# Layer 0's first steps by token tile: the first weight piece loaded between the two tiles

## The chip, the cores and the metric

The kernel runs on one core of a Trainium2 chip. Its time is the device time of one execution in microseconds (us). Before the change the median of three runs is 1185.62 us (1185.45 to 1185.66). The median is the number that a change is judged by.

## The reference

The program is a two-layer language-model body on 256 tokens of width 1024. Each layer normalizes the tokens (RMS norm with a gain per feature), multiplies them by one wide input matrix `w_in`, sends slices of the product through four mixers (an mLSTM, a latent attention, a gated linear attention and a convolution), fuses them with `w_out`, and adds a feed-forward part: dense in layer 0, a mixture of eight experts in layer 1. All of it is in float32.

```python
for l in range(DEPTH):
    z = rms_norm(h, norm1_g[l]) @ w_in[l]
    (m_qk, m_v, m_o, m_if, a_cq, a_ckv, a_kr,
     g_q, g_k, g_v, g_r, g_a, c_glu) = split_cols(z, IN_SPLITS)
    y = concat([mlstm_mixer(...), mla_mixer(...), gla_mixer(...), conformer_conv(...)])
    h = h + group_rms_norm(y, fuse_g[l], N_GROUPS) @ w_out[l]
    u = rms_norm(h, norm2_g[l])
    h = h + (swiglu(u, ...) if l % 2 == 0 else moe_ffn(u, ...))
return rms_norm(h, final_norm_g)
```

The change touches only the first line of layer 0: `rms_norm(h, norm1_g[0])` and the first columns of its product with `w_in[0]`.

## The kernel before, in words

The 256 tokens are two tiles of 128 (t = 0, 1); `h` holds them in SBUF. Every engine has its own program, written out by hand in order, and engines wait for each other by semaphores. Nothing reorders them: an instruction that waits holds all that stands behind it on its engine.

A float32 product is made of three products in a rounded format. Each operand is split into a high part and a low part. For weights, ScalarE (ACT) copies a piece from the ring of loaded pieces into `high` (`split_high`, L870) and VectorE (DVE) or GpSimd (POOL) subtracts to get `low` (L1353 on DVE, L675 on POOL). For tokens, the normalized tile `un` is transposed by TensorE (PE) into a PSUM bank in four groups of two blocks (L1947). ACT then writes `uTh` with the gain (L904) and DVE writes `uTl` (L1370), group by group (`tile_gains`).

`w_in` comes in pieces, in the order l0, l1, b, a, mq, mk, gqk, rg0, rg1, vo0, vo1. Pieces l0 and l1 hold the same 376 columns: l0 five of the eight blocks of 128 features, l1 the other three. For each token tile PE makes 15 matmuls of 376 columns with l0 and 9 with l1 (`half("l0", 0)` is tile 0 with l0, and so on; L2150 to L2152). Pieces b, a, mq, mk are feature-major: each half is 24 matmuls of 256 columns (L1965 to L1967) that need both tiles.

The order before, in layer 0, on each engine:

- SP issues the loads: x of tile 0, x of tile 1 (L545), then the pieces of `w_in`, each as two DMAs (L492). Ahead of piece 4 (mq) it waits for eleven small DMAs of POOL (`rows_in`).
- ACT: sum of squares and rstd of tile 0, then of tile 1 (`tile_rstd`, L885 to L890); gains of tile 0, groups 0 and 1; `high` of l0; gains of tile 0, groups 2 and 3; gains of tile 1; `high` of l1; `high` of b; three mask copies (L1011); `high` of a; copies of the first product (L1020, L1022); `high` of mq; the gates (L1026 to L1030).
- DVE: `normalize` of tile 0 and tile 1 (L1361); low gains of tile 0, groups 0 and 1; `low` of l0; the other low gains; `low` of l1; `low` of b.
- PE: the 8 transposes of tile 0, the 8 of tile 1, nine matmuls of the identity (L2125, which keep the engine active until the first weights are ready), `half("l0", 0)`, `half("l0", 1)`, `half("l1", 0)`, `half("l1", 1)`, two transposes of constants (L2252, L2253), then b, a matmul with `walpha` (L2267), small transposes, a, and the rest.
- POOL: constants, the small DMAs of `rows_in` and `gate_b`, then a wait for `norm_tr` to reach 8, which is the count of transposed groups of both tiles:

```python
pool.wait_ge(s["norm_tr"], steps_before(3 * l + 1))
pool.dma_start(walpha[:, :], gla_w_alpha[l]).then_inc(s["ukv_in"], 16)
```

Behind that wait stand five DMA issues (L698 to L702), the rotary angles (`angles`, L638 to L660: a chain of small operations in which nearly every one waits for the one before), and then `low` of piece a, `low` of mq and so on (`split_low`, L675). PE waits for `low` of a ahead of `half("a", 0)`.

The banks of the transposes are `START_BANKS[0]`; a bank is claimed again only when the reader of its last content is done.

Of the kernel before, what the change touches and what calls it, by code (L numbers as in the profile page):

```python
# [25 lines left out]
ACT = mybir.ActivationFunctionType  # L26
# [3 lines left out]
P = 128  # L30
# [104 lines left out]
def build(nc, x, positions, norm1_g, w_in, mlstm_conv_w, mlstm_conv_b, mlstm_gate_b,  # L135
# [25 lines left out]
    with ctx:  # L161
# [219 lines left out]
        UP_BANKS, GATE_BANKS = (0, 1), (4, 7)  # L381

        UP_FIRST, GATE_FIRST = (6, 3), (2, 5)
        START_BANKS = (((2, 0, 1, 4), (3, 5, 7, 6)), ((0, 1, 4, 7), (3, 4, 7, 0)))
        SPLIT_BANKS = ((0, 1, 4, 2), (0, 1, 4, 7))
        DENSE_ACC, MOE_ACC = ((2, 3), (5, 6)), ((2, 3),)

# [94 lines left out]
        def _(sp):  # L482
# [58 lines left out]
                                  w.rearrange("(k p) n -> p k n", p=P)[:, k0:k0 + 4, c * WIDE:c * WIDE + 256])  # L541
                                 for g, w in enumerate((wg, wu))], rounds)

            for t in range(TT):
                sp.dma_start(h[:, t, :], x[0, t * P:(t + 1) * P, :]).then_inc(s[f"x{t}_in"], 16)  # L545
            for p in range(N_IN):
                if p == 4:

                    sp.wait_ge(s["rows_in"], 16 * 11)
                load_in(0, p)  # L550
# [309 lines left out]
        def _(act):  # L860
# [11 lines left out]
            def tile_rstd(t, k=None, squares=un, halves=False):  # L872

                if halves:
                    for i in range(2):
                        act.wait_ge(s["h_ready"], 4 * k + 2 * t + i + 1)
                        at = slice(i * 512, (i + 1) * 512)
                        chain.done(act.activation(squares[:, t, at], h[:, t, at], ACT.Square, accum_out=ss[:, t, i:i + 1]))
                    chain.wait()
                    chain.done(act.activation(ss[:, t, 1:2], ss[:, t, 1:2], ACT.Copy, scale=1.0 / D, bias=EPS))  # L880
                    bias = ss[:, t, 1:2]
                else:
                    if k is not None:
                        act.wait_ge(s["h_ready"], 4 * k + 2 * t + 2)
                    chain.done(act.activation(squares[:, t, :], h[:, t, :], ACT.Square, accum_out=ss[:, t, 0:1]))  # L885
                    bias = epst[:, :]
                chain.wait()
                chain.done(act.activation(lnv[:, t, 0:1], ss[:, t, 0:1], ACT.Ln, bias=bias, scale=1.0 / D))
                chain.wait()
                act.activation(rstd[:, t, 0:1], lnv[:, t, 0:1], ACT.Exp, scale=-0.5).then_inc(s["rstd_ready"], 1)  # L890
# [7 lines left out]
            def tile_gains(k, first, t, banks, steps=range(4)):  # L898

                for g in steps:  # L900
                    act.wait_ge(s["norm_tr"], steps_before(k) + 4 * t + g + 1)
                    for i in range(2):
                        kd = 2 * g + i
                        last = act.activation(uTh[:, kd, t * P:(t + 1) * P], bank[banks[t][g]][:, i * P:(i + 1) * P],  # L904
                                              ACT.Copy, scale=col(first + kd))
                    last.then_inc(s["uth_ready"], 1)
# [63 lines left out]
            for l in range(DEPTH):  # L970
                n0 = LAYER_PIECES[l]
                def split_in(name):
                    split_high(n0 + IN_AT[name], width=in_width(name))
# [7 lines left out]
                if l:  # L981
                    split_in("l0")
                    act.preload_act_table_set(LN_EXP)
                    tile_rstd(0, 1, halves=True)
                    split_in("l1")
                    tile_gains(3 * l, NORM1 + KD * l, 0, START_BANKS[l])
                    tile_rstd(1, 1, halves=True)
                    n = n0 + IN_AT["b"]
                    act.wait_ge(loaded[SLOT_OF[n]], 32 * FILL_OF[n])
                    act.wait_ge(s["piece_used"], n - SPLIT + 1)  # L990
                    act.activation(high[:, n % SPLIT, 0:PIECE // 2], slot(n)[:, 0:PIECE // 2], ACT.Copy).then_inc(s["b_half"], 1)
                    tile_gains(3 * l, NORM1 + KD * l, 1, START_BANKS[l])
                    act.activation(high[:, n % SPLIT, PIECE // 2:], slot(n)[:, PIECE // 2:], ACT.Copy).then_inc(s["high_ready"], 1)
                else:
                    act.wait_ge(s["ident_ready"], 1)
                    for t in range(TT):
                        act.wait_ge(s[f"x{t}_in"], 16)
                        tile_rstd(t)
                    act.wait_ge(s["cols_ready"], 1)
                    tile_gains(0, NORM1, 0, START_BANKS[0], (0, 1))  # L1000
                    split_in("l0")
                    tile_gains(0, NORM1, 0, START_BANKS[0], (2, 3))
                    tile_gains(0, NORM1, 1, START_BANKS[0])
                    split_in("l1")
                if l:
                    split_in("a")
                else:
                    split_in("b")
                    act.wait_ge(s["consts"], 1)
                for out_, in_ in ((ident_r, ident), (mask_kr, mask_kt), (mask_qr, mask_qt)):  # L1010
                    last = act.activation(out_[:, :], in_[:, :], ACT.Copy)  # L1011
                last.then_inc(s["masks_ready"], 1)
                if l == 0:
                    split_in("a")
                else:

                    act.wait_ge(s["rows_written"], ZEROED)

                act.wait_ge(s["tile_done"], 3 * l + 1)
                act.activation(zl[:, 0, :], bank[PAIR_BANKS["l"][0]][:, 0:376], ACT.Copy).then_inc(s["zl_ready"], 1)  # L1020
                used("l1")
                act.activation(zl[:, 1, :], bank[PAIR_BANKS["l"][1]][:, 0:376], ACT.Copy).then_inc(s["zl_ready"], 1)  # L1022
                split_in("mq")

                act.wait_ge(s["gates_in"], l + 1)
                chain.done(act.activation(gab[:, :, :], gb[:, :, 4:8], ACT.Abs))  # L1026
# [319 lines left out]
        def _(dve):  # L1346
# [9 lines left out]
            def normalize(l, t):  # L1356

                dve.wait_ge(s["rstd_ready"], 4 * l + t + 1)
                for i in range(2):
                    at = slice(i * 512, (i + 1) * 512)  # L1360
                    dve.tensor_scalar(un[:, t, at], h[:, t, at], rstd[:, t, 0:1], None, ALU.mult).then_inc(s["un_ready"], 1)  # L1361

            def tile_gains(k, first, t, banks, steps=range(4)):

                for g in steps:
                    dve.wait_ge(s["uth_ready"], steps_before(k) + 4 * t + g + 1)
                    for i in range(2):
                        kd = 2 * g + i
                        at = slice(t * P, (t + 1) * P)
                        last = dve.scalar_tensor_tensor(  # L1370
                            out=uTl[:, kd, at], in0=bank[banks[t][g]][:, i * P:(i + 1) * P], scalar=col(first + kd),
                            in1=uTh[:, kd, at].bitcast(F32), op0=ALU.mult, op1=ALU.subtract)
                    last.then_inc(s["utl_ready"], 1)
# [57 lines left out]
            for l in range(DEPTH):  # L1431
# [7 lines left out]
                if l:  # L1439
                    split_in("l0")  # L1440
                    add_tile(0, DENSE_ACC[0], "dense_half", 1)
                    normalize(l, 0)
                    tile_gains(3 * l, NORM1 + KD * l, 0, START_BANKS[l], (0, 1))
                    add_tile(1, DENSE_ACC[1], "piece_used", DENSE0 + N_FFN)
                    tile_gains(3 * l, NORM1 + KD * l, 0, START_BANKS[l], (2, 3))
                    normalize(l, 1)
                    tile_gains(3 * l, NORM1 + KD * l, 1, START_BANKS[l])
                else:
                    dve.wait_ge(s["cols_tr"], 1)
                    dve.tensor_copy(cols[:, 2, :], bank[7][:, 0:P]).then_inc(s["cols_ready"], 1)  # L1450
                    normalize(0, 0)
                    normalize(0, 1)
                    dve.wait_ge(s["cols_ready"], 1)
                    tile_gains(0, NORM1, 0, START_BANKS[0], (0, 1))
                    split_in("l0")
                    tile_gains(0, NORM1, 0, START_BANKS[0], (2, 3))
                    tile_gains(0, NORM1, 1, START_BANKS[0])

                chain.done(dve.memset(vaug[:, :, :, DH:DH + 1], 1.0))
                if l:  # L1460
                    dve.wait_ge(s["moe_in"], 16)
                    dve.tensor_tensor(router[:, :, :], router[:, :, :], bc(cols[:, 0, NORM2 + KD:NORM2 + 2 * KD].unsqueeze(2), [P, KD, E]),
                                      ALU.mult).then_inc(s["router_ready"], 1)
                if l == 0:
                    split_in("l1")
                if l:

                    n = n0 + IN_AT["b"]
# [460 lines left out]
        def _(pe):  # L1929
# [184 lines left out]
            for l in range(DEPTH):  # L2114
# [3 lines left out]

                if l == 0:
                    start_transposes(0, 0)  # L2120
                    start_transposes(0, 1)

                    pe.wait_ge(*owner[0])
                    for _ in range(9):
                        pe.matmul(bank[0][:, 0:P], ident[:, :], ident[:, :], start=True, stop=True)  # L2125

                def half(name, i, reader=None, ahead_of_last=None):

# [113 lines left out]
                if l:  # L2242
                    half("l1", 0, ahead_of_last=lambda: start_transposes(l, 1, (0, 1)))
                    start_transposes(l, 1, (2, 3))
                half("l0", 1, ("zl_ready", 2 * l + 2))
                if l == 0:
                    half("l1", 0)
# [340 lines left out]
```

## Time and profile before

| what | value |
|---|---|
| median of three runs | 1185.62 us |
| the profiled execution | 1185.43 us |
| its span | 1183.5 us |
| PE busy | 1163.9 us, 98% of the span |
| DVE busy | 943.5 us, 80% |
| ACT busy | 835.4 us, 71% |
| POOL busy | 297.9 us, 25% |
| PE's share of the chain that ended last | 93% |
| first weight matmul (L2150) | starts at 13.39 us |

The span runs from the first to the last instruction of the profiled execution; the execution's own time is 1.93 us longer. The chain that ended last is followed backwards from the last instruction to what released it at each step. A row of the timeline gives the start, the length, the engine, the line, the operation and, in brackets, the idle time before it with what ended it; "x4" means four instructions merged in one row.

### The profile page before, as it was taken

The page shows a single profiled execution, that of the slowest core. Times are in us where ns is not written, and L with a number is a line of the kernel's source. Part 1 is how long each engine was busy: PE and PEld are TensorE (multiplying, and loading weights), DVE is VectorE, ACT ScalarE, POOL GpSimd, SP SyncE. Part 2 cuts the span into 40 slices and gives each one's busy share as a digit, 9 for nine tenths or more (in the row PEclk, how much of TensorE's full clock was granted, in tenths as well). Part 3 has the DMA queues.
Part 4 walks back from the last instruction along what each step waited for, and adds up shares of the span by engine and source line. Part 5 has one row for each costly group of instructions (what it writes and reads, how often), then busy time and mean ns, then how long its engine had stood idle before and what let it go on. Part 6 is the DMA issues. An engine that isn't in the chain of part 4 may idle for free.

```text
span 1183.5 us, 17063 instructions
## 1 busy us (share of the span) xinstructions
PE 1163.9 (98%) x5916; PEld 968.5 (82%) x5916; DVE 943.5 (80%) x868; ACT 835.4 (71%) x880; POOL 297.9 (25%) x301
## 2 busy tenths in 40 slices
PE   7999999999999999999999999999999999999996
PEld 7987888888888778888888888888888888888885
DVE  4875554455597579998899898899899899889997
ACT  7786634434768767777787777777777777778775
POOL 9976000000597654412003003003003003000000
PEclk9999999999999999999999999999999999999999
DMA  9544975625254499999999999999999999999971
GB/s 308 181 147 158 395 271 180 210 53 178 66 180 131 160 344 393 380 390 393 389 391 394 388 386 389 369 383 376 387 383 370 387 371 380 392 369 370 394 291 55
DMA packets 173846, 358.98 MB, mean 303 GB/s; under 512 B 15136, under 2 KB 46042, under 8 KB 173793
## 3 DMA queue, kind: packets, MB, share of 16 engines
q1 hardware_dynamic: 167600, 344.17, 80.0%
q0 software_dynamic: 6016, 13.84, 3.5%
q8 instruction: 32, 0.52, 0.2%
q10 hardware_dynamic: 176, 0.27, 0.1%
q14 instruction: 22, 0.17, 0.0%
HBM read 352.18 MB, written 9.70 MB: 306 GB/s over the span
## 4 chain that ended last, share of the span: by engine, by line
PE 93%; DVE 3%; ACT 2%; issue 1%; DMA 1%; SPq 0%; DVEq 0%; ACTq 0%
PE bank L2003 17%; PE bank L2005 17%; PE bank L2004 17%; PE bank L2023 8%; PE bank L2022 8%; PE bank L2021 8%; PE bank L2047 2%; PE bank L2150 2%; DVE low L1353 2%; PE bank L2152 2%; PE bank L2151 2%; PE bank L1965 1%; PE bank L1967 1%; PE bank L1966 1%; PE bank L2233 1%; PE bank L2235 1%
## 5 line engine op out<-in xcount | busy, mean ns | idle before, releaser
L1353 DVE TENSOR_TENSOR low<-ring,high 128x2048 fp32r<-128x2048 f32 (+1 forms) x301 | 684.0, 2286 | 116.0 <-ACT high L870 112.9
L870 ACT ACTIVATE high<-ring 128x2048 fp32r<-128x2048 f32 (+1 forms) x326 | 623.0, 1912 | 163.0 <-PE bank L2005 113.9
L2003 PE MATMUL bank<-high,uTh 128*128 128x512 f32 x880 | 347.5, 395 | 0.5 <-DVE low L1353 0.4
L2005 PE MATMUL bank<-high,uTl 128*128 128x512 f32 x880 | 343.3, 390 | 0.0
L2004 PE MATMUL bank<-low,uTh 128*128 128x512 f32 x880 | 342.8, 390 | 0.0
L2003 PEld LDWEIGHTS bank<-high,uTh 128*128 128x128 f32 x880 | 165.3, 188 | 36.1 <-DVE low L1353 1.6
L2005 PEld LDWEIGHTS bank<-high,uTl 128*128 128x128 f32 x880 | 165.1, 188 | 35.0
L2004 PEld LDWEIGHTS bank<-low,uTh 128*128 128x128 f32 x880 | 165.4, 188 | 33.0
L840 POOL DMA_INDIRECT expert_rows<-yrows,row_idx x7 | 10.4, 1488 | 505.8 <-ACT yrows L1268 505.8
L675 POOL TENSOR_TENSOR low<-ring,high 128x512 fp32r<-128x512 f32 (+1 forms) x67 | 84.6, 1296 | 196.1 <-ACT high L870 195.4
L2021 PE MATMUL bank<-high,moe_hTh 128*128 128x512 f32 x320 | 125.3, 391 | 0.0
L2023 PE MATMUL bank<-high,moe_hTl 128*128 128x512 f32 x320 | 124.8, 390 | 0.0
L2022 PE MATMUL bank<-low,moe_hTh 128*128 128x512 f32 x320 | 124.6, 389 | 0.0
L2023 PEld LDWEIGHTS bank<-high,moe_hTl 128*128 128x128 f32 x320 | 60.1, 188 | 12.6
L2021 PEld LDWEIGHTS bank<-high,moe_hTh 128*128 128x128 f32 x320 | 60.1, 188 | 12.5 <-issue 0.3
L2022 PEld LDWEIGHTS bank<-low,moe_hTh 128*128 128x128 f32 x320 | 60.1, 188 | 12.3
L834 POOL DMA_INDIRECT back<-token_rows,quad_idx x28 | 57.8, 2064 | 11.9 <-issue 6.4
L961 ACT ACTIVATE moe_hTh<-bank 128x512 fp32r<-128x512 f32 (+1 forms) x48 | 27.0, 562 | 46.2 <-PE bank L2047 46.2
L953 ACT ACTIVATE moe_sg<-bank 128x512 f32<-128x512 f32 (+1 forms) x48 | 27.0, 563 | 38.1 <-PE bank L2005 38.1
L683 POOL TENSOR_TENSOR low<-ring,high 128x512 fp32r<-128x512 f32 x32 | 42.6, 1364 | 19.9 <-ACT high L870 19.5
L1965 PE MATMUL bank<-uTh,high 128*128 128x256 f32 x160 | 46.2, 288 | 0.7 <-DVE bank L1553 0.7
L1490 DVE SCALAR_TENSOR_TENSOR cacc<-bank,cols,cacc 128x255 f32<-128x255 f32 (+29 forms) x120 | 45.7, 457 | 0.1
(416 smaller groups left out, 1404.3 us busy)
## 6 DMA issues: line engine op xcount, KB each, us to landing
ring<-in_moe_w_up_dram SPq DMA_DIRECT2D x176, 512.0 KB, 6.6
ring<-in_moe_w_gate_dram SPq DMA_DIRECT2D x176, 512.0 KB
ring<-in_moe_w_down_dram SPq DMA_DIRECT2D x176, 512.0 KB, 8.2
ring<-in_w_in_dram SPq DMA_DIRECT2D x36, 512.0 KB, 6.1
ring<-in_ffn_w_up_dram SPq DMA_DIRECT2D x22, 512.0 KB, 7.2
ring<-in_ffn_w_gate_dram SPq DMA_DIRECT2D x22, 512.0 KB
ring<-in_ffn_w_down_dram SPq DMA_DIRECT2D x22, 512.0 KB, 3.7
ring<-in_w_out_dram SPq DMA_DIRECT2D x16, 512.0 KB
```

The source lines that it names most:

```text
L675: last = pool.tensor_tensor(low[:, n % SPLIT, at], slot(n)[:, at], high[:, n % SPLIT, at].bitcast(F32), ALU.subtract)
L834: pool.indirect_dma_start(xrows_q[:, j, :], None, tokens_q[:, :], bass.IndirectOffsetOnAxis(quad_idx[:, j, n:n + 1], 0), bounds_check=8 * ...
L870: act.activation(high[:, n % SPLIT, 0:width], slot(n)[:, 0:width], ACT.Copy).then_inc(s["high_ready"], 1)
L1353: dve.tensor_tensor(low[:, n % SPLIT, 0:width], slot(n)[:, 0:width], high[:, n % SPLIT, 0:width].bitcast(F32), ALU.subtract).then_inc(s["l ...
L1490: ins = dve.scalar_tensor_tensor(out=cacc[:, c, shift:S], in0=src, scalar=w, in1=cacc[:, c, shift:S], op0=ALU.mult, op1=ALU.add)
L1965: pe.matmul(dst, ah, bh, start=first, stop=False)
L2003: pe.matmul(o, ah, bh, start=(kd == 0), stop=False)
L2004: pe.matmul(o, ah, bl, start=False, stop=False)
L2005: last = pe.matmul(o, al, bh, start=False, stop=(kd == KD - 1))
L2021: pe.matmul(o, ah, bh, start=(c == 0 and f == 0), stop=False)
L2022: pe.matmul(o, ah, bl, start=False, stop=False)
L2023: last = pe.matmul(o, al, bh, start=False, stop=(c == LAST and f == 1))
```

## The change

x of tile 1 is issued behind piece l0 on SP. ACT takes tile 0 alone first: its rstd, then `high` of l0, then all its gains; only then the rstd of tile 1, `high` of l1 and the gains of tile 1. DVE normalizes tile 1 between the low gains of tile 0, and `low` of l1 comes ahead of the last group of tile 1. PE transposes tile 1 between `half("l0", 0)` and `half("l0", 1)`; the nine identity matmuls follow the transposes of tile 0, into bank 1 and without a wait for a bank. In layer 0 the three mask copies move behind `high` of mq. POOL's program is not changed.

```diff
-        START_BANKS = (((2, 0, 1, 4), (3, 5, 7, 6)), ((0, 1, 4, 7), (3, 4, 7, 0)))
+        START_BANKS = (((0, 4, 3, 5), (7, 6, 0, 4)), ((0, 1, 4, 7), (3, 4, 7, 0)))
@@ SP
-            for t in range(TT):
-                sp.dma_start(h[:, t, :], x[0, t * P:(t + 1) * P, :]).then_inc(s[f"x{t}_in"], 16)
             for p in range(N_IN):
+                if p < TT:
+                    sp.dma_start(h[:, p, :], x[0, p * P:(p + 1) * P, :]).then_inc(s[f"x{p}_in"], 16)
@@ ACT
-                    for t in range(TT):
-                        act.wait_ge(s[f"x{t}_in"], 16)
-                        tile_rstd(t)
+                    act.wait_ge(s["x0_in"], 16)
+                    tile_rstd(0)
+                    split_in("l0")
                     act.wait_ge(s["cols_ready"], 1)
-                    tile_gains(0, NORM1, 0, START_BANKS[0], (0, 1))
-                    split_in("l0")
-                    tile_gains(0, NORM1, 0, START_BANKS[0], (2, 3))
+                    tile_gains(0, NORM1, 0, START_BANKS[0])
+                    act.wait_ge(s["x1_in"], 16)
+                    tile_rstd(1)
+                    split_in("l1")
                     tile_gains(0, NORM1, 1, START_BANKS[0])
-                    split_in("l1")
...
                 split_in("mq")
+                if l == 0:
+                    act.wait_ge(s["consts"], 1)
+                    mask_copies()
@@ DVE
                     normalize(0, 0)
+                    split_in("l0")
+                    dve.wait_ge(s["cols_ready"], 1)
+                    tile_gains(0, NORM1, 0, START_BANKS[0], (0, 1, 2))
                     normalize(0, 1)
-                    dve.wait_ge(s["cols_ready"], 1)
-                    tile_gains(0, NORM1, 0, START_BANKS[0], (0, 1))
-                    split_in("l0")
-                    tile_gains(0, NORM1, 0, START_BANKS[0], (2, 3))
-                    tile_gains(0, NORM1, 1, START_BANKS[0])
+                    tile_gains(0, NORM1, 0, START_BANKS[0], (3,))
+                    tile_gains(0, NORM1, 1, START_BANKS[0], (0, 1, 2))
+                    split_in("l1")
+                    tile_gains(0, NORM1, 1, START_BANKS[0], (3,))
@@ PE
                     start_transposes(0, 0)
-                    start_transposes(0, 1)
-
-                    pe.wait_ge(*owner[0])
+
                     for _ in range(9):
-                        pe.matmul(bank[0][:, 0:P], ident[:, :], ident[:, :], start=True, stop=True)
+                        pe.matmul(bank[1][:, 0:P], ident[:, :], ident[:, :], start=True, stop=True)
...
+                else:
+                    start_transposes(0, 1)
                 half("l0", 1, ("zl_ready", 2 * l + 2))
```

## Rows read from the trace of the kernel before

**Rows 1.** The chain of waits, 0 to 150 us: start us, us, what.

```profile
0.81 0.39 SPq L545
1.25 0.43 SPq L545
1.73 0.43 SPq L492
2.19 7.20 DMA ring<-in_w_in_dram
9.42 1.78 ACT high L870
11.22 2.13 DVE low L1353
13.39 0.44 PE bank L2150
...
117.57 0.87 PE bank L1947 x8
```

**Rows 2.** Waits of PE, 0 to 150 us: line <- awaited: total, times, longest.

```profile
PE bank L1957 <- ACT y L931: 0.8, 1, 0.8
PE bank L2150 <- DVE low L1353: 0.3, 1, 0.3
```

**Rows 3.** Tile h up to 15 us: time from issue to landing of its DMAs.

```profile
DMA to landing us min/median/max: 3.8/4.3/4.7
```

**Rows 4.** Timeline of ACT to 25 us (start, length, engine, line, operation).

```profile
6.25 0.20 ACT L890 ACTIVATE rstd<-lnv 128x1 f32<-128x1 f32 x1
6.36 1.04 ACT L885 ACTIVATE un<-h 128x1024 f32<-128x1024 f32 x1
8.10 0.63 ACT L904 ACTIVATE uTh<-bank,cols 128x128 fp32r<-128x128 f32 x2
11.10 3.19 ACT L904 ACTIVATE uTh<-bank,cols 128x128 fp32r<-128x128 f32 x12
14.10 1.23 ACT L870 ACTIVATE high<-ring 128x1128 fp32r<-128x1128 f32 x1
15.13 2.00 ACT L870 ACTIVATE high<-ring 128x2048 fp32r<-128x2048 f32 x1
23.68 1.92 ACT L870 ACTIVATE high<-ring 128x2048 fp32r<-128x2048 f32 x1 [1.23 <-DMA ring<-in_w_in_dram]
```

**Rows 5.** Timeline of DVE to 25 us.

```profile
13.26 0.60 DVE L1370 SCALAR_TENSOR_TENSOR uTl<-bank,cols,uTh 128x128 fp32r<-128x128 f32 x2
13.26 3.19 DVE L1370 SCALAR_TENSOR_TENSOR uTl<-bank,cols,uTh 128x128 fp32r<-128x128 f32 x12
16.37 1.32 DVE L1353 TENSOR_TENSOR low<-ring,high 128x1128 fp32r<-128x1128 f32 x1
17.61 2.30 DVE L1353 TENSOR_TENSOR low<-ring,high 128x2048 fp32r<-128x2048 f32 x1
```

**Rows 6.** Timeline of PE, to 30 us.

```profile
7.31 3.68 PE L1947 MATMUL bank<-ident,un 128*128 128x128 f32 x16 [0.78 <-DVE un L1361]
10.78 2.35 PE L2125 MATMUL bank<-ident 128*128 128x128 f32 x18
21.76 0.27 PE L2252 MATMUL bank<-ident,y 128*128 128x128 f32 x1
29.67 0.37 PE L1965 MATMUL bank<-uTh,high 128*128 128x256 f32 x1
```

**Rows 7.** Timeline of POOL, 12 to 30 us.

```profile
13.25 0.52 POOL L698 DMA_DIRECT2D walpha<-in_gla_w_alpha_dram  x1
15.94 0.24 POOL L638 CAST pos_f<-pos_i 128x2 f32<-128x2 int32 x1
16.60 3.39 POOL L644 TENSOR_SCALAR turn<-ang 128x32 f32<-128x32 f32 x2
16.60 1.18 POOL L644 TENSOR_SCALAR turn<-ang 128x32 f32<-128x32 f32 x1
...
24.36 1.29 POOL L675 TENSOR_TENSOR low<-ring,high 128x512 fp32r<-128x512 f32 x1
29.53 1.30 POOL L675 TENSOR_TENSOR low<-ring,high 128x512 fp32r<-128x512 f32 x1
```

More of the change, by code:

```diff
@@ L995, in _, with mask_copies @@
                     act.wait_ge(s["ident_ready"], 1)
-                    for t in range(TT):
-                        act.wait_ge(s[f"x{t}_in"], 16)
-                        tile_rstd(t)
+                    act.wait_ge(s["x0_in"], 16)
+                    tile_rstd(0)
+                    split_in("l0")
                     act.wait_ge(s["cols_ready"], 1)
-                    tile_gains(0, NORM1, 0, START_BANKS[0], (0, 1))
-                    split_in("l0")
-                    tile_gains(0, NORM1, 0, START_BANKS[0], (2, 3))
+                    tile_gains(0, NORM1, 0, START_BANKS[0])
+                    act.wait_ge(s["x1_in"], 16)
+                    tile_rstd(1)
+                    split_in("l1")
                     tile_gains(0, NORM1, 1, START_BANKS[0])
-                    split_in("l1")
+                def mask_copies():
+                    for out_, in_ in ((ident_r, ident), (mask_kr, mask_kt), (mask_qr, mask_qt)):
+                        last = act.activation(out_[:, :], in_[:, :], ACT.Copy)
+                    last.then_inc(s["masks_ready"], 1)
                 if l:
                     split_in("a")
+                    mask_copies()
+                    act.wait_ge(s["rows_written"], ZEROED)
                 else:
                     split_in("b")
[L1009 to L1013, printed above, removed]
                     split_in("a")
-                else:
-                    act.wait_ge(s["rows_written"], ZEROED)
                 act.wait_ge(s["tile_done"], 3 * l + 1)
@@ L1023, in _ @@
                 split_in("mq")
+                if l == 0:
+                    act.wait_ge(s["consts"], 1)
+                    mask_copies()
                 act.wait_ge(s["gates_in"], l + 1)
@@ L1463, in _ @@
                                       ALU.mult).then_inc(s["router_ready"], 1)
-                if l == 0:
-                    split_in("l1")
                 if l:
```

## Prediction

> **What bounds the kernel now.** I read the chain of waits first. It starts with SP's issues of x and of the first weight piece, then the landing of l0, then ACT's `high`, DVE's `low`, and from 13.39 us PE [rows 1]. Then PE's waits: up to 150 us, beside those ahead of the first transposes, there are only two, 0.3 us for `low` of l0 ahead of 13.39 and 0.8 us for ACT at L1957, near 99 us, and the latter hangs on PE's own work before it [rows 2]. So PE is dense from 13.39 us on, and what decides the change is how late PE is at each point it passes: a lateness is never made up, since no slack of PE's lies behind. The first eight transposes start at 7.31 us; the 48 weight matmuls (2 tiles x (15 + 9)) run from 13.39 to 21.76 us, where the transpose of constants begins [rows 1, 6], so 8.37 us, 0.174 us each. Piece a starts at 29.67 us [rows 6].
>
> The second thing to see is POOL. It issues `walpha` at 13.25 us, behind a wait on all eight transposed groups that was already met, and its `low` of a ends at 29.4 us: the `low` of mq starts at 29.53 [rows 7], about 0.1 us after it. PE starts a at 29.67 us. So POOL is only about 0.25 us ahead of PE there, though PE shows no wait.
>
> **The change part by part.**
>
> *Landing of l0.* x of tile 0 is issued at 0.81 and lands 3.8 us later, at 4.6; x of tile 1 is issued at 1.25 and lands 4.7 us later, at 5.95 [rows 1, 3]. Tile 1's x thus takes 1.35 us of the stream. With l0 in its place, l0's landing moves from 9.39 (2.19 + 7.20) to about 8.05 us. The least gain is that of the issue alone, 0.48 us earlier (1.73 less 1.25): landing 8.9. The largest I allow is 0.85 us beyond the stream's share, landing 7.2, if the slow part of l0's own 7.20 us does not recur. I take 8.05, since bytes ahead of it set it.
>
> *ACT and DVE to the first matmul.* `high` of l0 starts at 8.1 and `low` at 9.9 (1.80 after it, as 11.22 stands to 9.42). DVE is free for gains 2.04 us later (13.26 less 11.22), at 11.95; the first pair takes 0.60 [rows 1, 5]. ACT has written `uTh` of that group by then: it is free at 9.8 and a pair takes 0.63 [rows 4]. So the first matmul starts at 12.6 instead of 13.39: 0.8 us gained. Later groups follow at 0.52 us (3.11 us of starts for 12, two each) against 1.03 us that PE needs for each, so they cost nothing. The identity matmuls now start after 8 transposes instead of 16. In the trace 16 transposes take 3.47 us of starts, 0.217 each, where eight later in the kernel take 0.87, 0.109 each [rows 1, 6]: PE is at the lower of its two levels (1.2 GHz) there. The 18 identity instructions take 0.13 each, so the rise to 2.4 GHz lies in their beginning, about 11.1 us. With the same activity from 7.31 us on, 10 of the 18 identity instructions run slow and 8 at 0.11: they end at 12.05, hidden.
>
> *Tile 1 on PE's path.* The 15 matmuls of `half("l0", 0)` end near 15.3 (15 x 0.1725, and 0.1 us of start-up). Behind them are now the eight transposes, 0.87 us, to 16.2; before, they were ahead of 10.8 us and free. They must not wait for `un`: ACT's gains of tile 0 take eight times 0.25 us from 9.8 to 11.8 (12 in 3.00), rstd of tile 1 takes 1.74 (8.10 less 6.36) to 13.55, and DVE's normalization, which stands behind the gains that end at 13.5, is done at 14.5 [rows 4, 5]. x of tile 1 lands near 9.5 and is not late. Then PE needs `uTl` of tile 1's first group: the bank is ready at 15.7, ACT's pair 0.63, DVE's pair 0.60 and two hand-overs of 0.04: 17.0. PE idles 0.8 us. From there 15 + 9 + 9 matmuls and 0.1 us of start-up bring the transposes of constants to 22.8 instead of 21.76. `low` of l1 is ready: DVE ends it at 19.2, needed at 19.7. So PE is **1.05 us late** at b: 0.8 gained, 0.87 and 0.8 and twice 0.1 lost. The least for this gap is 0 (if gains ran ahead), the most 1.1.
>
> *b.* ACT's gains of tile 1 end at 17.7, `high` of b 2.0 us later, at 19.7; before it was done at 17.1 [rows 4]. `low` of b follows on DVE from 19.7 to 22.0 (2.30, rows 5); PE needs it at 22.9. Hidden.
>
> *POOL's wait.* The eighth group is now transposed at 16.35 (six transposes more and the last one's own length), not near 10.8. POOL, which came to this wait at 13.25, now stands until 16.35: **3.1 us**. Behind it: five issues, the angles, then `low` of a. The chain from `walpha` to the end of `low` of a is 16.17 us (13.25 to 29.42), and in it lie two stalls. The two L644 operations take 1.18 and about 2.1 us, where their like take 0.4, and each ends 0.1 us behind the end of a DVE `low` (17.69 and 19.91) [rows 5, 7]: while DVE subtracts with both inputs in SBUF, POOL's small operations stand. These two cost 2.5 us. In the new order the cast falls to 19.1, near the end of `low` of l1 (19.2); the two operations behind it bring POOL to 19.9, just into `low` of b (19.7 to 22.0). The first L644 stands until 22.1, the second runs free to 22.5. From the end of the second L644 (16.60 + 3.39) to the first L675 (24.36) it is 4.4 us [rows 7], so `low` of a starts at 26.9 and, 5.06 us long, ends at 31.95. PE would be at a at 29.67 + 1.05 = 30.7. It waits 1.25 us, and a starts **2.3 us late**. Bounds: with no stall of POOL at all `low` of a ends at 29.42 + 3.1 - 2.5 = 30.0 and PE is 1.05 late only; with the L644 pair split around `low` of b, one before and one after, it is 1.9.
>
> The Trainium skill ("SBUF — State Buffer", on the shared port pair) says that a tensor_tensor with two SBUF inputs on VectorE and a GpSimd operation that reads SBUF exclude each other, and that the second fully blocks until the first is done. The two L644 rows agree, with ends 0.1 us behind DVE's. By a reading in which the stalls are POOL's own and move along with it, `low` of a would end at 29.42 + 3.1 and a start 2.9 us late; by the page's it is the 2.3 above.
>
> *Small DMAs.* The five issues behind the wait, some 0.65 MB, now go 3.1 us later and share the stream with mq, which lands for ACT at 23.68 [rows 4] today. At worst mq is 1.8 us later. Then the gates and the mask copies (three, 0.2 us of starts each, now ahead of the gates: 0.6 us) make PE's small transposes up to 0.5 us late, all of it inside the 1.25 us that PE waits for a anyway. If that wait were gone, it would cost 0 to 0.5. The masks' leaving the place ahead of `high` of a gains nothing: that copy waits for PE.
>
> *Later.* Everything behind a hangs on PE. POOL is 2.5 us later than before, PE 2.3, and POOL has over 1 us in hand at its later hand-overs. **Sum:** -0.8 + 0.87 + 0.8 + 0.2 + 1.25 = +2.3 us. The profiled execution would take 1185.43 + 2.3 = 1187.7; it stood 0.2 us under the median, so the median comes to **1187.9 us**.
>
> **The rivals.**
>
> - *POOL is in time.* Its angles miss DVE's subtractions, or stall less. Then PE is only 1.05 us late: 1186.7. For it: only 2.5 us of stalls would have to shrink. Against: DVE's `low` of l1 and of b move by 2 us just as POOL does.
> - *l0 lands late (slower).* If its descriptors and not the bytes ahead set its landing, it lands at 8.9 and all times above move by 0.85: +3.15, 1188.8. For it: l0 takes 7.20 us from issue, more than x. It decides from a landing later than 8.15, where the loss passes 0.2%.
> - *The clock falls (slower).* PE now has two gaps, 0.5 and 0.8 us. If it went back to 1.2 GHz in one, and took as long to rise as at the start (7.31 to 11.1), half of 3.8 us is lost, 1.9 more less what hides in the wait for a: +3.5, 1189.1. Against: the gap of 0.3 us ahead of 13.39 did not do that [rows 2]. The Trainium skill ("TensorE: Matmul & The Clock Gate", on the clock gate) says the engine falls back after it has been idle; no row here shows so short an idleness enough.
> - *Faster: the gap closes.* l0 lands by 7.5, PE starts right behind the identity matmuls at 12.05, and tile 1's gains are ready behind its transposes. Then constants are at 12.05 + 8.4 + 0.87 = 21.35, 0.4 us sooner, and if POOL is in time too, 1185.2. It decides only when both the landing is 0.6 us earlier than I take it and the gap of 0.8 us is nothing; PE, ACT and DVE work in series there, which speaks against it.
> - *The landing is early but nothing else changes*: all times 0.5 us sooner, +1.8, 1187.4.
>
> **How the numbers follow.** Forecast 0.50, POOL in time 0.20, late landing 0.14, early landing 0.08, clock 0.05, faster 0.03. The middle of the forecast is spread by 0.5 us each way, since the landing is good to 0.3 and the meeting with `low` of b to 0.4. 0.2% is 2.37 us, 1187.99 (about what a measurement of this kernel can tell from no change). Of the forecast's 0.50, 0.22 lies above that; with late landing (0.13) and clock (0.05) slower has 0.40. Faster by over 0.2% would need more than the whole gain at the start: 0.02. Within: 0.58. The range goes from 1186.5, just under POOL in time, to 1188.9, just over the late landing.
>
> **What would show it.** The first L2150 near 12.6; eight L1947 between 15.3 and 16.2; a gap of 0.8 us and L2252 near 22.8; `walpha` issued near 16.4 instead of 13.25; one L644 about 2.2 us long ending behind `low` of b; the first L675 near 26.9; a wait of PE for POOL of 1.2 us ahead of a, which starts near 32.0. I am wrong if PE starts a without a wait, or if the first L2150 is not earlier than 13.0 or is earlier than 12.1.

## The result, and the profile after

The changed kernel takes 1188.3 us (median of 16 runs, 1188.05 to 1188.58); the kernel before took 1185.63 us beside it (16 runs). The ratio is 1.0021, 95% interval 1.0015 to 1.0028: 2.7 us or 0.22% slower. The profiled execution has a span of 1186.4 us, 2.9 more than before. The forecast was 1187.9 us, slower by 2.3. The range holds the measured time, which lies a little outside the 0.2% that the forecast had put just inside.

The waits of PE up to 150 us, in the kernel after (engine, line, awaited: total, times, longest) answer to [rows 2]:

```profile
PE bank L2152 <- DVE uTl L1374: 1.6, 2, 0.9
PE bank L1951 <- DVE un L1365: 1.0, 1, 1.0
PE bank L1969 <- POOL low L675: 0.8, 1, 0.8
PE bank L1961 <- ACT y L931: 0.8, 1, 0.8
PE bank L2152 <- ACT dec L1121: 0.3, 1, 0.3
```

Two waits of the weight matmuls on `uTl`, one on POOL and one on ACT are new. (Lines behind the SP block moved: L2152 was L2150, L1969 was L1965, L1951 was L1947, L1961 was L1957, L1374 was L1370, L1568 was L1564, L2256 was L2252.)

The timeline of ACT in the kernel after, for [rows 4]:

```profile
8.29 1.77 ACT L870 ACTIVATE high<-ring 128x1880 fp32r<-128x1880 f32 x1 [2.26 <-DMA ring<-in_w_in_dram]
9.96 2.16 ACT L904 ACTIVATE uTh<-bank,cols 128x128 fp32r<-128x128 f32 x8
11.97 1.11 ACT L885 ACTIVATE un<-h 128x1024 f32<-128x1024 f32 x1
15.94 2.18 ACT L904 ACTIVATE uTh<-bank,cols 128x128 fp32r<-128x128 f32 x8 [1.18 <-PE bank L1951]
```

The timeline of DVE, for [rows 5]:

```profile
10.09 2.12 DVE L1357 TENSOR_TENSOR low<-ring,high 128x1880 fp32r<-128x1880 f32 x1 [3.04 <-ACT high L870]
16.60 1.65 DVE L1374 SCALAR_TENSOR_TENSOR uTl<-bank,cols,uTh 128x128 fp32r<-128x128 f32 x6 [1.44 <-ACT uTh L904]
19.96 2.29 DVE L1357 TENSOR_TENSOR low<-ring,high 128x2048 fp32r<-128x2048 f32 x1
56.45 1.23 DVE L1568 CAST negm<-negm 4x256 fp32r<-4x256 f32 x1
```

That of PE, for [rows 6]; L1951 at 15.52 are tile 1's transposes, L2256 is the first transpose of constants, L1969 at 32.03 is the start of piece a:

```profile
6.65 1.97 PE L1951 MATMUL bank<-ident,un 128*128 128x128 f32 x8 [1.01 <-DVE un L1365]
8.42 3.52 PE L2127 MATMUL bank<-ident 128*128 128x128 f32 x18
12.87 0.41 PE L2152 MATMUL bank<-high,uTh 128*128 128x376 f32 x1 [0.94 <-DVE uTl L1374]
15.52 1.03 PE L1951 MATMUL bank<-ident,un 128*128 128x128 f32 x8
17.26 0.44 PE L2152 MATMUL bank<-high,uTh 128*128 128x376 f32 x1 [0.70 <-DVE uTl L1374]
23.04 0.27 PE L2256 MATMUL bank<-ident,y 128*128 128x128 f32 x1
32.03 0.39 PE L1969 MATMUL bank<-uTh,high 128*128 128x256 f32 x1 [0.84 <-POOL low L675]
65.89 0.47 PE L2152 MATMUL bank<-high,uTh 128*128 128x512 f32 x1 [0.31 <-ACT dec L1121]
```

The last of these rows, the first matmul of piece rg0, stood in the kernel before as:

```profile
63.05 0.40 PE L2150 MATMUL bank<-high,uTh 128*128 128x512 f32 x1
```

And that of POOL, for [rows 7]:

```profile
16.85 0.52 POOL L698 DMA_DIRECT2D walpha<-in_gla_w_alpha_dram  x1 [3.88 <-PE bank L1951]
19.53 0.23 POOL L638 CAST pos_f<-pos_i 128x2 f32<-128x2 int32 x1
20.20 2.44 POOL L644 TENSOR_SCALAR turn<-ang 128x32 f32<-128x32 f32 x2
26.98 11.37 POOL L675 TENSOR_TENSOR low<-ring,high 128x512 fp32r<-128x512 f32 x8
```

What the reader is to see: PE starts 0.5 us earlier (12.87 for 13.39) and is 1.28 us late at the transposes of constants (23.04 for 21.76). It is 2.36 us late at piece a (32.03 for 29.67), behind POOL. POOL stood 3.9 us in the wait that it had passed at once before. The first L644 stands through DVE's `low` of b: alone it takes 2.14 us and ends at 22.34, 0.1 behind it. From a to the first rg0 matmul the lateness grows by another 0.5 us, to 2.84 (65.89 for 63.05). From 102 us to the last matmul it stays at 2.95 us.

### The profile page after: what moved, and what is told of

Same layout as the page of the kernel before. It is cut to its first block, busy times and chain, and to the rows that moved or that the text cites. A ratio compares the mean times of both kernels' runs of the same rounds, so it can differ in the third digit from the quotient of the medians.

```text
span 1186.4 us, 17063 instructions
## 1 busy us (share of the span) xinstructions
PE 1165.0 (98%) x5916; PEld 969.0 (82%) x5916; DVE 944.0 (80%) x868; ACT 835.4 (70%) x880; POOL 296.8 (25%) x301
## 4 chain that ended last, share of the span: by engine, by line
PE 91%; DVE 4%; ACT 2%; issue 1%; POOL 1%; DMA 1%; DVEq 0%; SPq 0%; ACTq 0%; POOLq 0%
PE bank L2007 17%; PE bank L2009 17%; PE bank L2008 16%; PE bank L2027 8%; PE bank L2026 8%; PE bank L2025 7%; PE bank L2051 2%; PE bank L2152 2%; DVE low L1357 2%; PE bank L2154 2%; PE bank L2153 2%; PE bank L2235 1%; PE bank L1969 1%; PE bank L2237 1%; PE bank L2236 1%
## 5 line engine op out<-in xcount | busy, mean ns | idle before, releaser
L675 POOL TENSOR_TENSOR low<-ring,high 128x512 fp32r<-128x512 f32 (+1 forms) x67 | 84.9, 1300 | 196.2 <-ACT high L870 195.4
L2025 PEld LDWEIGHTS bank<-high,moe_hTh 128*128 128x128 f32 x320 | 60.1, 188 | 12.6 <-issue 0.3
L1969 PE MATMUL bank<-uTh,high 128*128 128x256 f32 x160 | 46.2, 289 | 1.6 <-POOL low L675 0.8
```

Source lines behind the costliest of these rows:

```text
L675: last = pool.tensor_tensor(low[:, n % SPLIT, at], slot(n)[:, at], high[:, n % SPLIT, at].bitcast(F32), ALU.subtract)
L1969: pe.matmul(dst, ah, bh, start=first, stop=False)
L2025: pe.matmul(o, ah, bh, start=(c == 0 and f == 0), stop=False)
```

## The experiments

All were timed in five rounds beside the kernel before, whose median was 1185.7 us in each set. "Changed kernel" is 1188.3, from its own set of runs. Where an engine is said to be late, it is against the profiled execution of the kernel before, and one execution of each kernel was profiled.

**POOL's angles ahead of its wait.**

```diff
+                if l == 0:
+                    angles()
                 pool.wait_ge(s["norm_tr"], steps_before(3 * l + 1))
                 pool.dma_start(walpha[:, :], gla_w_alpha[l]).then_inc(s["ukv_in"], 16)
...
-                if l == 0:
-                    angles()
```

> The changed kernel, but in layer 0 POOL computes the rotary angles ahead of its wait for the eight transposed groups, so that the wait (it idles 3.9 us there) is filled. Theory (two losses: 1.3 us from tile 1 on PE's path, and about 1.5 us because POOL's wait makes low of piece a late and shifts POOL against DVE): PE does not wait for POOL at a; a starts at 29.7 + 1.3 = 31.0 us, the end of the program is 1.3 us later than before, 1.3 to 1.8 if POOL's other hand-overs shift; about 1187.0. Rival (PE's path alone, POOL only follows): no difference to the changed kernel, 1188.3.

Measured: 1186.81 us (ratio to before 1.0009, 1.0 to 1.0018). PE has no wait for POOL and none for ACT at 65 us; it is 1.4 us late at the transposes of constants and still 1.4 at the end of the program. In POOL's timeline the two L644 take 0.51 us together, since no subtraction of DVE falls on them; the 1.16 us of L660 stand through `low` of l1:

```profile
13.60 0.51 POOL L644 TENSOR_SCALAR turn<-ang 128x32 f32<-128x32 f32 x2
18.53 1.16 POOL L660 TENSOR_SCALAR ang<-ang 128x64 f32<-128x64 f32 x1
22.51 10.22 POOL L675 TENSOR_TENSOR low<-ring,high 128x512 fp32r<-128x512 f32 x8
```

The theory holds: 1.5 of 2.7 us go with POOL's wait, and what is left is PE's own path.

**The other way round: only POOL late, in the kernel before.**

```diff
+                if l == 0:
+                    pool.wait_ge(s["utl_ready"], 8)
                 pool.wait_ge(s["norm_tr"], steps_before(3 * l + 1))
```

> The kernel before, with one added wait: in layer 0 POOL waits for the eighth low gain group (16.4 us) where it went on at 13.25. PE, ACT and DVE have their old order. Theory: POOL issues walpha near 16.7, 3.4 us late; the stall by DVE's low of b (17.6 to 19.9) now falls on the first operation of the angles instead of on the two L644, so part of the lateness is given back; low of a ends near 31.0 and a starts near 31.1 instead of 29.7: 1.4 us slower, up to 2.0 if POOL's shift also hits DVE's small operations later; 1187.0 to 1187.6. Rival (POOL has slack and the whole loss is PE's): 1185.6, no change.

Measured: 1186.85 us (1.001, 1.0001 to 1.0019), 1.15 us slower with PE, ACT and DVE in their old order, just under what was expected. Its landing of l0 was 0.34 us later in the profiled execution, so of the 1.0 us by which PE was late at a (30.67), 0.66 is POOL's; by the first rg0 matmul (64.50) another 0.45 has come on top. The stall moved to the cast, as expected (0.53 us instead of 0.24, and the L644 pair takes 0.51):

```profile
17.07 0.52 POOL L700 DMA_DIRECT2D walpha<-in_gla_w_alpha_dram  x1 [3.80 <-DVE uTl L1372]
19.75 0.53 POOL L638 CAST pos_f<-pos_i 128x2 f32<-128x2 int32 x1
20.71 0.51 POOL L644 TENSOR_SCALAR turn<-ang 128x32 f32<-128x32 f32 x2
25.59 9.74 POOL L675 TENSOR_TENSOR low<-ring,high 128x512 fp32r<-128x512 f32 x7
```

Its waits of PE show the same two as the changed kernel:

```profile
PE bank L1967 <- POOL low L675: 0.4, 1, 0.4
PE bank L2152 <- ACT dec L1119: 0.3, 1, 0.3
```

**Both tiles of x first.**

```diff
+            for t in range(TT):
+                sp.dma_start(h[:, t, :], x[0, t * P:(t + 1) * P, :]).then_inc(s[f"x{t}_in"], 16)
             for p in range(N_IN):
-                if p < TT:
-                    sp.dma_start(h[:, p, :], x[0, p * P:(p + 1) * P, :]).then_inc(s[f"x{p}_in"], 16)
```

> The changed kernel, but both tiles of x are loaded ahead of piece l0, as before; the orders of PE, ACT and DVE stay changed. Theory: l0 is ready for ACT near 9.4 instead of 8.3 us, and all of the start follows by that 1.1 us: 1189.4. Rival (the start is bound by something else, the identity matmuls or the transposes): 0 to 0.3 us against the changed kernel, 1188.3 to 1188.6.

Measured: 1191.38 us (1189.77 to 1192.76), 3.1 over the changed kernel and more than the landing explains: in the profiled execution, 3.3 over, `high` of l0 started at 10.1 us, 1.8 later. The table by stretch (us, busy time and count per engine, granted clock, DMA) shows the rest:

```profile
11.00:13.00 2.00, 1.07 (x8) 0.88 (x7) 1.09 (x1) 2.00 (x6) 2.00 (x4) 1.00 1.12 340
13.00:16.00 3.00, 1.31 (x4) 1.34 (x5) 3.00 (x9) 2.94 (x9) 0.06 (x1) 0.78 1.11 338
16.00:19.00 3.00, 3.00 (x13) 2.97 (x13) 0.98 (x4) 0.58 (x1) 0.00 (x0) 0.65 0.77 199
```

The granted clock is 0.78 and 0.65 of full: PE was back at 1.2 GHz for part of each, after it had stood idle for 2.6 us ahead of the first weight matmul (14.69). My forecast had this as a rival for the changed kernel, where it did not come; here it came.

**The same with twenty identity matmuls.**

```diff
-                    for _ in range(9):
+                    for _ in range(20):
```

> The changed kernel with both tiles of x ahead of piece l0 (as in the run that came to 1191.4, in which the clock fell behind a gap of 2.9 us), now with twenty identity matmuls instead of nine, which end near 14.5 us. Theory (of that run's 3.1 us over the changed kernel, 1.8 is the later landing and 1.3 or more the clock): no slow stretch between 14.7 and 18.1, 1189.5 to 1190.1. Rival (the landing alone made the 3.1): 1191.4.

Measured: 1190.03 us, 1.35 less than without them; the clock stays at full:

```profile
13.00:16.00 3.00, 2.98 (x22) 2.82 (x21) 3.00 (x10) 2.94 (x7) 0.30 (x1) 1.00 1.11 342
16.00:19.00 3.00, 2.29 (x17) 2.03 (x16) 1.56 (x7) 1.82 (x8) 0.77 (x2) 1.00 0.72 176
```

It is 1.7 us over the changed kernel. `high` of l0 starts 1.37 us later (9.66 for 8.29), against 1.35 in the forecast. The first weight matmul is 1.38 us later (14.25), so the twenty matmuls, which end just there, hold nothing up in this execution; the other 0.3 us or so of the 1.7 were not traced.

**No identity matmuls.** The loop of nine is taken out of the changed kernel.

> The changed kernel without its nine identity matmuls, so that PE is idle from 8.5 to 12.9 us. Theory (PE needs the activity to be at 2.4 GHz when the weights come): the first 15 or more matmuls take 0.31 instead of 0.172 us each, 2.1 us or more; POOL's wait and all behind it follow: 1190.4 to 1191.8. Rival (the activity does not matter): 1188.3.

Measured: 1190.84 us, 2.5 us over the changed kernel. The first fifteen weight matmuls, from 12.99 to 17.83 us, follow each other at 0.31 us (0.17 in the changed kernel) and take 2.2 us more. The clock column reads 1.00 all the same. So it does in the changed kernel and the one before where transposes follow at 0.22 us, and there too the spacing is what tells the level:

```profile
9.00:13.00 4.00, 0.01 (x1) 0.04 (x1) 2.79 (x4) 4.00 (x10) 4.00 (x8) 1.00 1.11 345
13.00:16.00 3.00, 3.00 (x10) 3.00 (x11) 2.28 (x8) 1.82 (x5) 0.12 (x1) 1.00 1.12 340
```

Ten matmuls in 3 us, all of weights, where the changed kernel had twenty, the last few of them tile 1's short transposes:

```profile
13.00:16.00 3.00, 3.00 (x20) 2.97 (x21) 2.16 (x7) 1.76 (x6) 0.00 (x0) 1.00 1.11 335
```

**The mask copies back in their place** (between `high` of b and `high` of a on ACT).

> The changed kernel, with the three mask copies back between high of b and high of a on ACT. Theory: they cost nothing in either place, since high of a waits for PE near 20.2 us and the gates have room: 1188.3, within 0.2 us. Rival (their new place ahead of the gates makes the small transposes or the gates late and takes part in the loss): 0.3 to 0.6 us faster than the changed kernel.

Measured: 1188.34 us. They cost nothing in either place.

**The last half microsecond: the copy of negm on ACT.**

```diff
-                act.activation(negm[0:4, :], mrun[:, :], ACT.Copy, scale=-1.0).then_inc(s["negm_ready"], 1)
+                chain.done(act.activation(negm[0:4, :], mrun[:, :], ACT.Copy, scale=-1.0))
+                chain.wait()
+                act.activation(negm[64:68, :], negm[0:4, :].bitcast(F32), ACT.Copy).then_inc(s["negm_ready"], 1)
...
-                dve.tensor_copy(negm[64:68, :], negm[0:4, :].bitcast(F32))
```

> The changed kernel; the copy of four rows of negm (L1568 on VectorE, 0.66 us in the kernel before and 1.2 us in the changed one, where it meets a subtraction of POOL) is made by ACT instead, in both layers. Theory (the last half microsecond of the loss, between a and the first rg0 matmul near 65.9 us, comes from that copy standing behind POOL): the wait of 0.3 us for ACT near 65 us is gone and the copy's own 0.66 us with it: 0.5 us faster than the changed kernel, 1187.8, up to 0.7 with layer 1. Rival (the wait at 65 us has another cause): 1188.3.

Measured: 1187.96 us, 0.34 less. PE's wait for ACT at 65 us is gone, and the lateness of 2.4 us at a (32.03) is still 2.4 at the first rg0 matmul (65.42). The gain is a little less than the 0.5 expected. That copy took 0.66 us in the kernel before and 0.72 with the angles first, neither of which has the wait, and 1.2 us in the changed kernel, in the kernel before with POOL late and with the masks back, which all have it. So the step from copy to wait is shown.

Why the copy is longer can be read beside POOL's subtractions. DVE's copy and the subtraction that POOL is in when it starts, in the kernel before:

```profile
53.31 1.27 POOL L675 TENSOR_TENSOR low<-ring,high 128x512 fp32r<-128x512 f32 x1
54.07 0.66 DVE L1564 CAST negm<-negm 4x256 fp32r<-4x256 f32 x1
```

In the changed kernel POOL's begins at 56.26:

```profile
56.26 1.27 POOL L675 TENSOR_TENSOR low<-ring,high 128x512 fp32r<-128x512 f32 x1
```

The copy ends 0.15 us behind the subtraction in both: 54.73 behind 54.58, and 57.68 behind 57.53. In all twelve profiled kernels in which DVE makes this copy it ends 0.14 to 0.16 us behind the subtraction that was running when it started, and it takes from 0.58 to 1.24 us. So the copy stands until POOL's subtraction is done, in the kernel before too; only the moment at which it starts differs.

**Tile 1's transposes inside half l0 0.** With the angles first, two of the four groups go ahead of the fourth feature block:

```diff
+                            if l == 0 and name == "l0" and i == 0 and k == 3:
+                                start_transposes(0, 1, (0, 1))
...
-                    start_transposes(0, 1)
+                    start_transposes(0, 1, (2, 3))
```

> The changed kernel with POOL's angles ahead of its wait (as in the run with the angles first, 1186.8) and, in addition, the first two groups of tile 1's transposes ahead of the fourth feature block of half l0 0, so that ACT and DVE prepare them while PE still multiplies tile 0. Theory (of the 1.3 us of PE's path, about 0.9 is the gap in which PE waits for uTl of tile 1 behind its transposes, the rest the transposes themselves less the earlier start): the gap of 0.98 us near 16.4 closes, b starts 0.9 us earlier, 1185.9. Rival (ACT and DVE are the bound of this stretch, so the wait only moves to low of l1): 0 to 0.3 us, 1186.5 to 1186.8.

Measured: 1188.77 us (1186.88 to 1191.25), a miss. The gap near 16.4 closed, and the transposes of constants start at 22.25 us, 0.9 earlier than with the angles first. But the small weights, issued behind the angles, came too late. POOL's timeline and the landing of its `ukv` (KB, us to landing):

```profile
19.63 2.22 POOL L660 TENSOR_SCALAR ang<-ang 128x64 f32<-128x64 f32 x1
...
24.05 0.60 POOL L704 DMA_DIRECT2D ukv<-in_mla_w_ukv_dram  x1
```

```profile
ukv<-in_mla_w_ukv_dram POOLq DMA_DIRECT2D x1, 256.0 KB, 6.9
```

24.05 + 6.9 = 30.95. PE's matmul with `walpha` waits for all five small weights. It starts at 31.09, after 2.3 us of idle time, and then the clock is down:

```profile
31.00:34.00 3.00, 2.91 (x11) 2.00 (x12) 0.48 (x1) 1.15 (x3) 3.00 (x4) 0.52 1.06 390
34.00:38.00 4.00, 4.00 (x21) 4.00 (x20) 3.82 (x6) 3.94 (x6) 3.99 (x6) 0.50 0.77 235
```

**Tile 1's transposes inside half l0 0 as before, POOL's order as in the changed kernel, and `low` of a on DVE.** The edit beside that of the transposes:

```diff
+                if l:
                     split_low("a")
                 split_low("mq")
... (DVE, behind split_in("b") in layer 0)
+                    split_in("a")
```

> The changed kernel with tile 1's first transposes ahead of the fourth feature block (as in the run with the transposes inside, but POOL's order as in the changed kernel, so that its small weights are issued first) and low of a on VectorE in layer 0. Theory (all of the loss is POOL's wait and the gap at tile 1): the gap of 1.0 us near 16.4 closes and PE never waits for POOL's low of a: 0.3 us over the kernel before, 1186.0. Rival (with POOL 3.6 us late its next hand-overs, mq or the rotary rows, bind instead): 1187 or more.

Measured: 1186.9 us (1.0011, 1.0002 to 1.002), 1.4 less than the changed kernel, but 0.9 over what was expected and near the rival. PE has neither the gap nor a wait for POOL, though POOL's cast now stands 2.15 us and L640 2.17 us in DVE's subtractions:

```profile
19.31 2.15 POOL L638 CAST pos_f<-pos_i 128x2 f32<-128x2 int32 x1
21.54 2.17 POOL L640 TENSOR_TENSOR ang<-invf,pos_f 128x32 f32<-128x32 f32 x1
```

PE is 0.15 us late at the transposes of constants and at a, and 0.5 at its last matmul. The rival, in which a later hand-over of POOL binds instead, does not show: up to 150 us PE has no wait for POOL. The other 0.8 us of the profiled run are the last store, 4.3 us from issue to landing instead of 3.4. Why it takes longer in this kernel stays open.

**Shortening the start of the kernel before.** Tile 1's order put aside: l0 is split in two parts (1128 and 752 columns), PE starts on the first, and three identity matmuls do for nine. In the first version POOL makes `low` of a ahead of the angles. Of the edit, ACT's part (DVE subtracts in the same two parts):

```diff
-                    split_in("l0")
+                    act.wait_ge(loaded[SLOT_OF[0]], 32)
+                    act.activation(high[:, 0, 0:1128], slot(0)[:, 0:1128], ACT.Copy).then_inc(s["b_half"], 1)
+                    act.activation(high[:, 0, 1128:1880], slot(0)[:, 1128:1880], ACT.Copy).then_inc(s["high_ready"], 1)
```

> The kernel before (both tiles first), but high and low of piece l0 are made in two parts of 1128 and 752 columns, PE starts on the first, three identity matmuls instead of nine, and POOL makes low of a ahead of the angles. If the start is bound by the serial landing, high, low (9.4, 11.2, 13.3), then DVE starts on the first part near 10.6 and PE near 12.0: 1.4 us earlier, and nothing behind it is in the way once POOL has a early: 1184.3 to 1184.6. Rival (another chain takes over at once: the gates behind mq, which lands at 23.7, or ckvT): 0.3 us or less gained, 1185.3. Third case: with fewer identity matmuls the clock falls or rises later, and it is slower, 1186 to 1187.

Measured: 1186.35 us, slower by 0.6 (1.0006, 0.9997 to 1.0015, an interval that holds no change), a miss. b starts at 20.77 us, 1.1 earlier, but POOL's rotary rows, now behind everything, take it all back. At the first rg0 matmul PE is 0.4 us late; the last store is slow here too (4.2 us):

```profile
PE bank L2230 <- POOL ktok L732: 1.3, 1, 1.3
PE bank L2160 <- DVE low L1458: 1.3, 1, 1.3
```

In the second version POOL keeps its old order and DVE makes `low` of a in layer 0.

> The kernel before with l0 made in two parts and three identity matmuls (as in the run of that name, whose first weight matmul was 1.2 us earlier and which then lost more than that to a wait of 1.3 us for POOL near 48 us), but POOL's angles back in their place and low of a made by VectorE in layer 0, which is idle there. Theory: both hand-overs of POOL, at a and at the head transposes, are in time, and the 1.1 us gained at b reach the end: 1184.6. Rival (the next chain, the gates behind mq or the landing of the small weights, takes them): 1185.4 or more.

Measured: 1184.32 us (0.9987, 0.9978 to 0.9996): 1.35 us faster than the kernel before and 4 us faster than the changed one. PE's waits up to 150 us:

```profile
PE bank L1956 <- DVE un L1365: 0.8, 1, 0.8
PE bank L1966 <- ACT y L933: 0.8, 1, 0.8
PE bank L2163 <- DVE low L1460: 0.3, 1, 0.3
```

Three identity matmuls are only just enough. In this profiled execution the second and third weight matmul follow 0.48 and 0.31 us behind the one before, where the first version has 0.27 and 0.17. The transposes of constants start 0.7 us earlier than in the kernel before, where the first version and the next one have 1.1 to 1.2.

With the copy of negm on ACT as well:

> The run before it (l0 in two parts, low of a on VectorE) with the copy of negm on ACT as well. Theory: if the meeting of that copy with POOL costs here too, 0.3 to 0.6 us faster than the run before it, 1184.1; if it doesn't meet there, equal to it within 0.2 us.

Measured: 1184.06 us (0.9987, 0.9978 to 0.9997), 0.26 less than without it, inside the 0.3 or so by which the runs of either spread. Between the two profiled executions 0.4 us are there at the transposes of constants already, and 0.45 at the first rg0 matmul, so nothing shows that the copy cost anything here.

## Why the prediction was right, step by step

- *Landing of l0.* Forecast 8.05 us; `high` starts at 8.29, so about 8.27 (1.73 + 6.54). In the seven profiled kernels with both tiles of x first, `high` of l0 starts between 9.42 and 10.11 us, the middle one at 9.66; in the seven with l0 in between it is 8.05 to 8.41, the middle one 8.29. The middles differ by 1.37 us, and the forecast had 1.35. The profiled execution of the kernel before is the earliest of its seven. This fits its time, 0.2 us under the median, and PE's 2.95 us, where the medians differ by 2.7. That it is x's bytes that l0 no longer waits for was only argued: of the 1.12 us between the two profiled executions 0.46 is the earlier issue and 0.66 the shorter time from issue to landing, and no run tells the two causes apart.
- *First matmul.* 12.6 forecast, 12.87 measured: 0.2 us is the landing, the rest lies between DVE's first low gain and PE.
- *Tile 1 on PE's path.* Forecast +1.05 at the constants, measured +1.28. The transposes start at 15.52 (15.3) and the next weight matmul follows at 17.26: 0.87 us for the transposes and 0.87 of gap, for a forecast of 0.87 and 0.8. From the first weight matmul to the constants it is 10.17 us for 8.37 before, 1.80 lost where 1.87 was forecast. So the excess at the constants is all in the first matmul.
- *POOL's wait.* Forecast 3.1 us, measured 3.6 (16.85 for 13.25), part of it 0.3 us between the last transpose's end and POOL's issue, for which I had no row. The rest came as forecast: L644 stands through `low` of b, the first L675 is at 26.98 (26.9), piece a at 32.03 (32.0), 2.36 us late (2.3). The extra half microsecond did no harm because the end of DVE's subtraction, not POOL's own start, set when the angles went on: the L644 pair took 2.44 us instead of 3.39 and gave back 0.95 of the 3.6. By the other reading of the stalls, in which they are POOL's own and move along, a would have been 2.9 us late; it was not, and the 2.95 at the end have another source. One size was wrong: the pair takes 0.51 us where nothing holds it up (with the angles first, and in the kernel before with POOL late), so its stalls before were 2.9 us and not 2.5. Only the bound without any stall hangs on that, 29.6 instead of 30.0. The two runs that move POOL alone confirm the wait from both sides.
- *Small DMAs and masks.* Nothing, as forecast.
- *Later.* This step failed. It said that everything behind a hangs on PE and that POOL has over 1 us in hand at its later hand-overs. No hand-over of POOL's was late, but DVE's copy of negm took 0.57 us longer, PE waited for ACT at 65.9 us and lost 0.5 us. The term was 0 in the sum; it measured 0.48 us, and with 0.1 us near 100 us, whose cause stays open, the profiled execution comes to 2.95 instead of 2.3. The same meeting costs 0.45 us in the kernel before with POOL late.
- *The rivals.* POOL in time is what the run with the angles first shows, 1186.8 for a forecast of 1186.7. The clock did not fall where PE stood idle for 0.94, 0.70 and 0.84 us, nor in the run with the copy of negm on ACT, where the first of these was 1.73; it fell behind 2.6 us. The identity matmuls end ahead of the first weight matmul in every profiled kernel of the changed order that has them. But the same eighteen instructions take 2.7 us in one and 3.9 in another, so the moment at which the clock rises is not the same from one to the next. A late landing did not come.

The sum of 2.3 stood just under the 2.37 that make 0.2%, and the measured 2.7 just over. The path of the loss was the forecast one up to a; the half microsecond that carried it over came from the term that the sum had put at nothing.

## What to carry to other kernels

When work is moved later on one engine, look for every counter that the moved work raises, on all engines: here a semaphore counted to 8 by both tiles' transposes held POOL, which the change does not touch, for 3.6 us. A long small-operation chain that needs nothing of the awaited data belongs ahead of such a wait, and DMA issues that someone needs soon belong ahead of the chain. Splitting one serial copy-and-subtract in two gave more at the start (1.1 us at b) than reordering the tiles, but it reached the end (1.35 us) only once the next late engine, POOL, had been relieved.

## What the runs showed that I had not expected

A shift of one engine by half a microsecond against another can cost that much 30 us later: DVE's copy of 4 x 256 numbers takes between 0.58 and 1.24 us, by how far POOL's subtraction has come when it starts. A wait of PE of 2.3 us in mid-kernel (until 31.09 us) was followed by 6.8 us at 1.2 GHz. The runs of that kernel spread over 4.4 us; that the clock makes this spread is likely but not shown, since only one of them was profiled. And with the same load order of x and l0, `high` of l0 started between 9.4 and 10.1 us in the seven kernels that have it.
